# Outer products of the sample tokens: one f16 pass over 96 stacked rows instead of an fp32 matmul

## What is computed

```python
s_new = exp(b_last)[..., None] * s0 + einsum('bshk,bshv->bhkv', k * exp(b_last[:, None] - b), v)     # HGRN2
s_new = exp(c * log_gamma) * s0 + einsum('bshk,bshv->bhkv', k * k_dec[None, :, :, None], v)          # retention
```

## Time and profile before

| what | value |
| --- | --- |
| median of 3 runs | 1769.54 us (1766.88 to 1772.71) |
| span of the profiled execution | 1765.4 us |
| busy share of the span | PE 90%, PEld 72%, DVE 53%, ACT 37%, POOL 9% |
| chain that ended last | PE 76%, DVE 10%, ACT 6%, issue 4%, queues 4% |

### The profile page before, as it was taken

How to read it: one execution, slowest core, us unless ns; L and a number is a source line. 1 busy time by engine, 2 the same in 40 slices (tenths; PEclk the granted TensorE clock), 3 DMA queues, 4 the chain that set the end, 5 groups by cost and what they waited for, 6 DMA issues and landing times.

```text
span 1765.4 us, 31743 instructions
## 1 busy us (share of the span) xinstructions
PE 1585.4 (90%) x12187; PEld 1263.6 (72%) x12187; DVE 930.3 (53%) x1493; ACT 657.9 (37%) x936; POOL 154.2 (9%) x126
## 2 busy tenths in 40 slices
PE   4699999998879999999957999999896999999994
PEld 3577777776658888878745777777674888887883
DVE  5766744443575555533266767444366555553334
ACT  3635423232263433422154544233235443333223
POOL 3111110000020000000030111100002000000002
PEclk8789889998989999999978989999987999999997
DMA  5121231220312233223321222222121323322321
GB/s 185 51 62 51 73 109 62 84 73 26 96 50 94 95 95 95 73 79 90 97 66 48 73 73 73 76 85 73 50 74 47 96 95 95 95 80 71 98 65 51
DMA packets 175036, 137.86 MB, mean 78 GB/s; under 512 B 5064, under 2 KB 169192, under 8 KB 174776
## 3 DMA queue, kind: packets, MB, share of 16 engines
q1 hardware_dynamic: 168192, 113.46, 21.1%
q0 software_dynamic: 5408, 18.60, 3.1%
q10 hardware_dynamic: 1372, 4.95, 0.8%
HBM read 124.91 MB, written 12.07 MB: 78 GB/s over the span
## 4 chain that ended last, share of the span: by engine, by line
PE 76%; DVE 10%; ACT 6%; issue 4%; DVEq 3%; ACTq 1%; DMA 1%; SPq 0%
PE ACC L506 60%; PE SCR L619 2%; PE SCR L536 2%; PE OT L627 2%; ACT WH L825 1%; PE SCR L657 1%; DVE X L1189 1%; PE OT L679 1%; DVE Z L1220 1%; PE OT L595 1%; DVE Fb L1202 1%; DVE WL L1149 1%; DVEq L1259 1%; PE SCR L722 1%; PE OT L594 1%
## 5 line engine op out<-in xcount | busy, mean ns | idle before, releaser
L506 PE MATMUL ACC<-XH,WH 128*128 128x280 f16 x2432 | 503.7, 290 | 74.7 <-DVE XL L1192 43.1
L506 PE MATMUL ACC<-XL,WH 128*128 128x280 f16 x2432 | 502.6, 289 | 0.0
L506 PE MATMUL ACC<-XH,WL 128*128 128x280 f16 x2432 | 502.2, 289 | 0.0
L506 PEld LDWEIGHTS ACC<-XH,WH 128*128 128x128 f16 x2432 | 237.4, 101 | 158.7 <-DVE XL L1192 45.9
L1149 DVE SCALAR_TENSOR_TENSOR WL<-stage,WH 128x2048 f16<-128x2048 f32 (+1 forms) x116 | 245.9, 2120 | 180.8 <-ACT WH L825 169.1
L506 PEld LDWEIGHTS ACC<-XL,WH 128*128 128x128 f16 x2432 | 243.4, 100 | 58.8
L506 PEld LDWEIGHTS ACC<-XH,WL 128*128 128x128 f16 x2432 | 243.5, 100 | 58.4
L825 ACT ACTIVATE WH<-stage 128x2048 f16<-128x2048 f32 (+1 forms) x116 | 204.8, 1765 | 103.0 <-PE ACC L506 85.7
L506 PE MATMUL ACC<-shared,WH 128*128 128x280 f16 x1408 | 225.4, 283 | 0.2
L506 PEld LDWEIGHTS ACC<-shared,WH 128*128 128x128 f16 x1408 | 137.6, 98 | 30.7 <-issue 0.8
L506 PE MATMUL ACC<-shared,WL 128*128 128x280 f16 x704 | 141.3, 283 | 0.0
(11 more groups left out here) (241 smaller groups left out, 1870.7 us busy)
## 6 DMA issues: line engine op xcount, KB each, us to landing
stage<-in_w_in_dram SPq DMA_DIRECT2D x64, 512.0 KB, 4.8
stage<-in_w_a_dram SPq DMA_DIRECT2D x44, 512.0 KB, 4.2
stage<-in_w_b_dram SPq DMA_DIRECT2D x44, 512.0 KB, 4.6
stage<-in_w_down_dram SPq DMA_DIRECT2D x32, 384.0 KB, 3.1
stage<-in_w_down_dram SPq DMA_DIRECT2D x32, 320.0 KB, 3.4
out_dram<-shared POOLq DMA_DIRECT2D x16, 512.0 KB, 3.4
stage<-in_w_o_dram SPq DMA_DIRECT2D x16, 512.0 KB, 3.9
shared<-in_state_hgrn_dram POOLq DMA_DIRECT2D x8, 512.0 KB, 5.8
```

Source lines behind the costliest of these rows:

```text
L506: last = mm(ACC[:, acc, h, 0:HALF], lhs, x[:, xk + k, h * HALF:(h + 1) * HALF], start=begin, stop=end)
```

## The change

The keys and values of the sample tokens become f16, each as a high and a low part, and three products (high by high, low by high, high by low) are stacked on 96 contraction rows of one f16 matmul. For that the 32 sample columns of KE and V stand three times side by side in SBUF, the transposes give 96 rows, ACT writes the high part of all of them to KV3, and DVE overwrites one third of the keys and one third of the values by the low part, from the same PSUM bank. POOL's masked copy VX now reads KV3 and has 96 rows of f16; it waits for the low parts (`kv_ready`). A scale of 8 on keys and values is taken out in DVE's add. The fp32 values that `sample_output` needs go to a tile of their own, VTS. The diff, cut to its core:

```diff
-        VX = sb("VX", [TS, DEC_BATCH, P])
-        KVTS = sb("KVTS", [TS, 2, P])
+        VX = sb("VX", [3 * TS, DEC_BATCH, P], F16)
+        KV3 = sb("KV3", [3 * TS, 2, P], F16)
+        VTS = sb("VTS", [TS, P])
...
+        def thrice(src):
+            return src[:, TP:TP + 3 * TS]
+        def copies(src):
+            return src[:, T:T + 2 * TS].rearrange("p (n t) -> p n t", n=2)
+        def twice(src):
+            return src[:, TP:T].unsqueeze(1).to_broadcast([P, 2, TS])
...
-                pool.wait_ge(tok_ready, hh + 1)
-                nc.gpsimd.tensor_tensor(VX[:, :, :], KVTS[:, 1:2, :].to_broadcast([TS, DEC_BATCH, P]), bcast(seqm[0:TS, :], P),
+                pool.wait_ge(kv_ready, hh + 1)
+                nc.gpsimd.tensor_tensor(VX[:, :, :], KV3[:, 1:2, :].to_broadcast([3 * TS, DEC_BATCH, P]), bcast(seqm[0:3 * TS, :], P),
...
-                            last = nc.tensor.transpose(SCR[0:TS, bank, i * P:(i + 1) * P], src[:, TP:T], ident)
+                            last = nc.tensor.transpose(SCR[0:3 * TS, bank, i * P:(i + 1) * P], thrice(src), ident)
...
-                mm(SCR[:, bank, :], KVTS[:, 0, :], VX[:, 4 * n:4 * n + 4, :].rearrange("p b v -> p (b v)"),
+                mm(SCR[:, bank, :], KV3[:, 0, :], VX[:, 4 * n:4 * n + 4, :].rearrange("p b v -> p (b v)"),
-                mm(cols_, KVTS[:, 1, :], PTSS[:, :], start=True, stop=False, skip_group_check=True)
+                mm(cols_, VTS[:, :], PTSS[:, :], start=True, stop=False, skip_group_check=True)
...
+                if buf is V:
+                    f(copies(V), ACC[:, c, 1, HALF - TS:HALF].unsqueeze(1).to_broadcast([P, 2, TS]), ACT.Copy, scale=INV_W)
...
-                f(KVTS[:, :, :], SCR[0:TS, 0, 0:2 * P].rearrange("p (n v) -> p n v", n=2), ACT.Copy).then_inc(scr_read[0], 1)
+                f(VTS[:, :], SCR[0:TS, 0, P:2 * P], ACT.Copy)
+                f(KV3[:, :, :], SCR[0:3 * TS, 0, 0:2 * P].rearrange("p (n v) -> p n v", n=2), ACT.Copy,
+                  scale=KV_SCALE).then_inc(kv_hi, 1)
                 act.drain().then_inc(tok_ready, 1)
...
-                f(KVTS[:, 0, :], SCR[0:TS, 0, 2 * P:3 * P], ACT.Copy, scale=tab[0:TS, ds(cols["k_dec_s"][0] + p, 1)])
-                f(KVTS[:, 1, :], SCR[0:TS, 0, 3 * P:4 * P], ACT.Copy).then_inc(scr_read[0], 1)
+                f(VTS[:, :], SCR[0:TS, 0, 3 * P:4 * P], ACT.Copy)
+                f(KV3[:, 0, :], SCR[0:3 * TS, 0, 2 * P:3 * P], ACT.Copy, scale=tab[0:3 * TS, ds(cols["k_dec_s"][0] + p, 1)])
+                f(KV3[:, 1, :], SCR[0:3 * TS, 0, 3 * P:4 * P], ACT.Copy, scale=KV_SCALE).then_inc(kv_hi, 1)
...
+                tt(copies(KE), twice(Fb), twice(T3), ALU.mult)
+                tt(copies(KE), twice(T1), twice(T2), ALU.add)
...
-                    tt(w, w, SCR[:, bank, :], ALU.add).then_inc(scr_read[bank], 1)
+                    stt(out=w, in0=SCR[:, bank, :], scalar=INV_KV, in1=w, op0=ALU.mult, op1=ALU.add).then_inc(scr_read[bank], 1)
+            def low_sample(hh, at_, key_scale):
+                dve.wait_ge(kv_hi, hh + 1)
+                for n, rows_, scale in ((0, slice(2 * TS, 3 * TS), key_scale), (1, slice(TS, 2 * TS), KV_SCALE)):
+                    last = stt(out=KV3[rows_, n, :], in0=SCR[rows_, 0, at_ + n * P:at_ + (n + 1) * P], scalar=scale,
+                               in1=KV3[rows_, n, :], op0=ALU.mult, op1=ALU.subtract)
+                last.then_inc(scr_read[0], 1)
+                dve.drain().then_inc(kv_ready, 1)
```

`low_sample` is called by DVE at the very start of `rt_a`, ahead of the five score jobs, and in groups that carry an HGRN2 head right behind `split_lo(1, j)`, ahead of `hg_gate` or, in group 4, ahead of `rt_key`:

```diff
                 split_lo(1, j)
+                if sample is not None:
+                    sample()
                 if kind == 0:
                     hg_gate(l, head, tile)
```

More of the change, by code:

```diff
@@ L54 @@
 INV_W = 1.0 / W_SCALE
+KV_SCALE = 8.0
+INV_KV = 1.0 / KV_SCALE ** 2
 C = 96
@@ L139, in const_tables @@
     put("mask32", causal)
-    put("seq", tok[:, None] // DEC_SEQ == np.arange(DEC_BATCH)[None, :])
+    put("seq", np.tile(tok[:, None] // DEC_SEQ == np.arange(DEC_BATCH)[None, :], (3, 1)))
     log_g = np.log1p(-np.exp2(-5.0 - np.arange(HEADS)))
@@ L150, in const_tables @@
     put("k_dec", np.where(left >= 0, np.exp(np.maximum(left, 0) * log_g[None, None, :]), 0.0) * root)
-    put("k_dec_s", np.exp((DEC_SEQ - 1 - tok % DEC_SEQ)[:, None] * log_g[None, :]) * root)
+    put("k_dec_s", np.tile(np.exp((DEC_SEQ - 1 - tok % DEC_SEQ)[:, None] * log_g[None, :]) * root * KV_SCALE, (3, 1)))
     put("gamma4", np.broadcast_to(np.exp(DEC_SEQ * log_g), (P, HEADS)))
@@ L213, in hybrid_decoder_step @@
         DK, DQ = sb("DK", [P, TP]), sb("DQ", [P, TP])
-        Fb, T1, T2, T3, B, Q, QS, QD, KE, E, V, G = (
-            sb(n, [P, T + 2]) for n in ("Fb", "T1", "T2", "T3", "B", "Q", "QS", "QD", "KE", "E", "V", "G"))
+        Fb, T1, T2, T3, B, Q, QS, QD, E, G = (
+            sb(n, [P, T + 2]) for n in ("Fb", "T1", "T2", "T3", "B", "Q", "QS", "QD", "E", "G"))
+        KE, V = sb("KE", [P, T + 2 * TS]), sb("V", [P, T + 2 * TS])
         at = [0]
@@ L648, in rest_transposes @@
                         nc.tensor.transpose(SCR[0:TAIL, 0, n * P:(n + 1) * P], src[:, 4 * P:TP], ident)
-                        last = nc.tensor.transpose(SCR[0:TS, 0, (2 + n) * P:(3 + n) * P], src[:, TP:T], ident)
+                        last = nc.tensor.transpose(SCR[0:3 * TS, 0, (2 + n) * P:(3 + n) * P], thrice(src), ident)
                     last.then_inc(scr_full, 1)
@@ L1382, in states @@
                     hg_states(l, p, s)
-                return (lambda: hg_scores(l, p, s)), states, None, (lambda: hg_d(l, p)), (lambda: sample_states(l, p, s))
+                return ((lambda: hg_scores(l, p, s)), states, None, (lambda: hg_d(l, p)), (lambda: hg_sample(l, p)),
+                        (lambda: sample_states(l, p, s)))
             def rt_a(l, p, scr):
                 hh = l * 2 * HEADS + HEADS + p
+                low_sample(hh, 2 * P, tab[2 * TS:3 * TS, ds(cols["k_dec_s"][0] + p, 1)])
                 bank = 1
@@ L1429, in rt_stages, with group @@
                     s.job(b)
-                return (lambda: rt_a(l, p, s)), (lambda: rt_b(l, p, s)), (lambda: rt_c(l, p, s)), (lambda: rt_d(l, p))
-            def group(l, g, head, kind, stages=(None,) * 4, mixed=None, after_hgrn=False):
-                a, b, c, d, *steps = stages
+                return (lambda: rt_a(l, p, s)), (lambda: rt_b(l, p, s)), (lambda: rt_c(l, p, s)), (lambda: rt_d(l, p)), None
+            def group(l, g, head, kind, stages=(None,) * 5, mixed=None, after_hgrn=False):
+                a, b, c, d, sample, *steps = stages
                 j, tile = l * SLOT_UNITS + g, l * TILES + 4 * g
@@ L1524, in _ @@
                 out_gate((l + 1) * 2 * HEADS - 1)
-                for stage_ in rt_stages(l, HEADS - 1):
+                for stage_ in rt_stages(l, HEADS - 1)[:4]:
                     stage_()
```

4 lines of the change are left out of this document (3 added, 1 removed).

## The result

The changed kernel takes 1752.93 us (median of 4 runs, 1751.11 to 1753.05) against 1770.35 us for the kernel before in the same comparison (4 runs, 1766.88 to 1772.71): a ratio of 0.9904, 95% interval 0.9892 to 0.9916. The profiled executions differ by 14.1 us of span: in every run on record the time is 1.5 to 2.7 us above the span, so the profiled execution of before (1765.4) is the quickest of its four.

What follows compares the result with a forecast made beforehand. PE was taken to bound the kernel, waiting for ACT, DVE and POOL before the outer products in groups 1 to 3. Gains of 1.8 + 1.5 + 4.2 less 2.8 gave 4.7 us: 1769.5 to 1764.8, range 1756 to 1775.

Steps and rivals of the forecast that it cites:

- Groups 1 to 3: Six HGRN2 heads, both layers: three half-clock heads gain 0.7 us each, three warm ones lose 0.1 each; 1.8 us gained.
- PE stays at half clock until 125.1: HGRN2 heads with half-clock products: clock return left in place, so tiles going on 1.45 us earlier are worth 0.7.
- clock term: Retention heads: the added 0.95 us wait lets two more heads fall to a lower clock, 2.8 us lost.
- The sum: Whole kernel: 1.8 + 1.5 + 4.2 - 2.8 = 4.7 us off the profiled execution.
- Group 4: HGRN2 group, twice: 1.15 us delay and 1.2 work replace 3.12 us; 0.75 gained each, 1.5 in all.
- Retention heads: Eight heads: 1.55 us gained, 0.95 lost to bank 0, last of each layer 0.3 net; 4.2 together before the clock loss.
- A low part: DVE, ahead of bank 0 and VX: 128 columns from PSUM take 0.347 us each, 0.69 for two.
- L1202's successor: DVE in groups 1 to 3: a sign of being right was L1202 still ending 0.6 us behind POOL.
- the 0.22 us that the prediction asked of them: PE's new products: a sign of being right was 32 records of L619 of about 0.22 us each.
- A: Rival on POOL: the masked product takes half its time with f16, removing groups 1 to 4's delay; 1756 us, chance 0.17.
- B: Rival on PE: longer waits cool it, all three warm HGRN2 heads turn cold at 4.7 us each; 1779 us, chance 0.20.

Runs made afterwards that it cites:

- without the delay: Changed kernel without DVE's low-part step and the waits for it, so VX and bank 0 wait only for ACT: 1731.67 us, ratio 0.9793 to before.
- low parts from SBUF: Changed kernel with ACT copying the sample tokens in fp32 on 96 rows to SBUF, DVE making the low parts from there: 1740.49 us, ratio 0.9837 to before.
- the longer wait: Changed kernel with one more DVE memset (128 x 1024) ahead of VX's release in six HGRN2 heads and two others: 1773.08 us, ratio 1.0025 to before.

## Why the prediction was wrong

**The failed step is the clock of the HGRN2 heads**, in "Groups 1 to 3". The prediction moved the tiles of a cold head 1.45 us forward, left the return of the clock where it had been ("PE stays at half clock until 125.1"), and so took half of 1.45; the second fall of a cold head, behind that point, had no price at all. Its clock term was a loss of 2.8 us, in the retention heads alone. The runs showed that the product moves the clock: without the delay it alone takes 13.9 us off the clock's price in the HGRN2 stretches. In a cold head full clock came back 22.7 us behind the copy and was lost once more for 3.4; after, it is back at 19.1 to 19.3 in five of the six heads and stays to the next copy. Over the six heads of groups 1 to 3 the time at 1.2 GHz behind the first product fell from 49.8 to 29.6 us, worth 10.1. Groups 1 to 3 gave 10.8 us, where 1.8 was foreseen.

**Work and waiting were sized nearly right.** The sum held about 22 for the product and 14 for the delay; PE's work fell by 21.2, and its idle time grew by 17.2. The clock was to cost 2.8 more and costs 8.0 less. That difference of 10.8 is more than the whole miss (14.1 us of span against 4.7).

The text had read the chain up to the products. Behind them it runs on PE for 30.8 to 35.5 us without a wait, in heads with the same work, and the clock's price lay open in this spread of 4.6 us.

**Group 4** gave 3.2 us for both layers together, 1.5 foreseen (2.8 in layer 0, 0.5 in layer 1).

**Retention heads.** Foreseen 4.2 - 2.8 = 1.4 gained, measured 2.0 lost. The product was sized right. Chain of the kernel after, first retention head:

```profile
281.55 0.32 PE SCR L635
281.87 0.72 PE ACC L522 x6
282.59 0.22 PE SCR L635
```

That is 1.26 us from the first product to the end of the second, 1.15 foreseen, with 0.22 for a pass. Without the delay the eight heads gain 13.0 (11.9 by the text's terms). With it, PE's work falls by 9.3, its idle time grows by 5.6 (8 x 0.95 = 7.6 foreseen), and the clock costs 5.7 more (2.8 foreseen). So the clock was undersized here, and its sign was right. The waits themselves are small:

```profile
274.30 0.67 PE L673 MATMUL SCR<-QD,KE 128*128 128x240 f32 x2 [0.87 <-DVE KV L1328]
```

and such rows sum to 3.2 us over all heads. The last retention head of layer 1, with no head behind it, runs from 1241.61 to 1273.47 in after at a mean granted clock of 0.77, and takes 31.9 us; with low parts from SBUF it takes 28.0 at 0.87, with the same work (busy time by clock is 24 us in both), and before the change 29.6 at 0.85. How much of the clock's 5.7 is the delay's doing stays open, since the same retention code took 299.5 to 308.7 us in the runs above.

**Sizes that held.** A low part takes 0.28 us, or 0.35 with the scale from a table, against 0.347; from copy to first product it is 0.9 to 1.2 us more in groups 1 to 3 (0.95 foreseen, bounds 0.8 to 1.2) and 1.3 in group 4 (1.15 foreseen); L1202's successor takes 1.30 us and ends 0.6 behind POOL, as before, so it is still POOL that sets its end. The records of L635 do not show the 0.22 us that the prediction asked of them (456 ns in the mean): neighbouring records overlap, and the pace is in the chain shown for the retention heads. Of the 4.1 us by which the profiled span lay below the median, 2.7 were that execution's being the quickest.

**The rivals.** A falls: VX takes 1887 ns in f16 on 96 rows, 1886 before. The Trainium skill (GPSIMD Engine Reference, side-by-side cycle accounting) paces a two-input instruction by element on a shared port, and these rows agree. B had the right event and the wrong price. Of the six heads of groups 1 to 3 five now fall to 1.2 GHz in PE's wait, two of them warm before, and one right behind the products, where the warm ones fell before. The Trainium skill (TensorE: Matmul & The Clock Gate, HAM oscillation) has it that gaps between matmul bursts throttle the engine again; the trace agrees in these five heads, and the two heads that kept full clock over a wait of 4.0 and 3.7 us show that such a gap need not do it. But B charged each turned head 4.7 us, a price read off heads whose next work was fp32; with f16 work behind the wait the three warm heads became 0.4 to 0.5 us longer.

Open: what decides when the clock falls, and for how long, in heads of the same kernel (before: 43.8 and 48.4 in turn; the longer wait: 45.0 to 49.6). The runs show that these lengths differ by the clock, not what sets it. The 2.1 us outside the stretches were not followed.

## What to carry to other kernels

Follow the chain past the change, up to the point where the loop repeats. Where it stays on one engine without a wait, that engine's work and its clock are the length, and two passes of the loop with the same work and different lengths (35.5 and 30.8 us here) show what the clock is worth before anything is built. Count half clock only where work lies under it: the part of it in PE's wait cost nothing here. Of a change of PE's work behind a wait, ask also what kind of work it leaves there: ten f16 passes and two fp32 matmuls of about equal time left different clocks here. An operand split into high and low parts costs little in itself, and more where it holds a shared PSUM bank: one fp32 copy on all the rows frees the bank, and the low parts can be made where the engine stands idle (here 12 us of 1753, of which the runs show 4.5 to be the bank's).

## What the runs showed of the hardware

At the lower clock, 3.78 us of fp32 matmuls kept PE there one stretch longer than 4.45 us of f16 passes did (0.50 against 0.97 in the windows above; 10.2 us against 6.8 in four and six heads). The prediction had counted both as work alike. A wait of PE of 3.7 us came with half clock in some heads and with full clock in others. ACT's copy of 96 rows by 256 columns takes 0.36 us, where that of 32 rows took 0.37, and POOL's product on 96 rows is no longer than on 32; two half products on POOL take 2.03 us against 1.89 for one.
